# Head rounds of a gated delta net: the convolutions' border terms on GpSimd, one ScalarE operation a panel, and the second transposes in another PSUM bank

## What is computed

```python
def _dn_inputs(p, dn_conv):
    y = jax.nn.silu(_dwconv(p[6], dn_conv)).astype(jnp.float32)      # 3 taps along the tokens, padding 1
    q, k, v = [t.reshape(B, T, DN_HEADS, DN_DIM) for t in jnp.split(y, 3, axis=-1)]
    return (_l2norm(q), _l2norm(k), v) + ...

def _gated_delta_chunked(q, k, v, g, beta, s0):
    ...
    a_mat = jnp.where(strict, jnp.einsum('nbhid,nbhjd->nbhij', kb, kc) * decay_mat, 0.0)
    sol = lax.linalg.triangular_solve(a_mat, rhs, left_side=True, lower=True, unit_diagonal=True)
    ...                      # then a scan over the chunks, for both directions
```

## Time and profile before

| | us |
|---|---|
| time, median of 3 runs (2981.7 to 2985.14) | 2983.79 |
| the profiled execution | 2986.58 |
| its span, first to last instruction | 2984.8 |
| TensorE busy | 2930.5 (98%) |
| VectorE busy | 1928.6 (65%) |
| ScalarE busy | 1460.3 (49%) |
| GpSimd busy | 354.9 (12%) |
| one round, first layer / second layer | 44.85 / 39.2 |

### The profile page before, as it was taken

The page is one execution under the profiler, slowest core; times in us unless marked ns, Lnnn a source line. Parts: engine busy times, 40 slices in busy tenths (PEclk is TensorE's granted clock), DMA queues, the critical chain, the costliest instruction groups (busy, mean ns, idle before and its releaser), DMA issues.

```text
span 2984.8 us, 50450 instructions
## 1 busy us (share of the span) xinstructions
PE 2930.5 (98%) x17768; PEld 2467.4 (83%) x17768; DVE 1928.6 (65%) x3479; ACT 1460.3 (49%) x2497; POOL 354.9 (12%) x272
## 2 busy tenths in 40 slices
PE   7999999999999999999999999999999999999998
PEld 5888888888887788888888888888788889799887
DVE  4777767766535834445665766657777766766777
ACT  5222267777546732224222342223788867644654
POOL 0000024444101000001000000000244421000000
PEclk9999999999999999999999999999999999999999
DMA  7544521111222022233444434444221114155554
GB/s 285 190 168 176 178 93 50 63 63 50 68 95 71 22 99 93 97 106 101 176 151 158 170 123 172 162 141 169 86 71 63 63 63 165 44 176 176 163 183 155
DMA packets 101845, 365.63 MB, mean 122 GB/s; under 512 B 11216, under 2 KB 12880, under 8 KB 101584
## 3 DMA queue, kind: packets, MB, share of 16 engines
q1 hardware_dynamic: 98384, 353.02, 34.6%
q10 hardware_dynamic: 3328, 10.81, 1.0%
HBM read 362.67 MB, written 1.11 MB: 122 GB/s over the span
## 4 chain that ended last, share of the span: by engine, by line
PE 90%; ACT 4%; DVE 3%; issue 2%; DMA 1%; SPq 0%; DVEq 0%; POOL 0%; ACTq 0%; POOLq 0%
PE bank L2123 69%; PE bank L2102 4%; PE bank L2104 2%; PE bank L2681 1%; PE bank L2421 1%; PE bank L2463 1%; PE bank L2396 1%; PE bank L2654 1%; PE bank L2667 1%; PE bank L2393 1%; PE bank L2474 1%; ACT ada_raw L944 1%; PE bank L2453 1%; PE bank L2486 1%; PE bank L2484 1%
## 5 line engine op out<-in xcount | busy, mean ns | idle before, releaser
L584 ACT ACTIVATE whi<-raw 128x1024 fp32r<-128x1024 f32 x518 | 546.7, 1058 | 991.4 <-PE bank L2123 964.1
L2123 PE MATMUL bank<-uh,whi 128*128 128x512 f32 (+1 forms) x2688 | 999.9, 372 | 8.3 <-DVE lmat L1725 2.0
L2123 PE MATMUL bank<-uh,wlo 128*128 128x512 f32 (+1 forms) x2688 | 982.2, 365 | 0.0
L2123 PE MATMUL bank<-ul,whi 128*128 128x512 f32 (+1 forms) x2688 | 972.9, 362 | 0.0
L1310 DVE TENSOR_TENSOR wlo<-raw,whi 128x1024 fp32r<-128x1024 f32 x476 | 583.4, 1226 | 368.6 <-ACT whi L584 353.4
L2123 PEld LDWEIGHTS bank<-uh,whi 128*128 128x128 f32 x2688 | 508.4, 189 | 97.4 <-issue 26.4
L2123 PEld LDWEIGHTS bank<-uh,wlo 128*128 128x128 f32 x2688 | 508.1, 189 | 72.8 <-issue 3.4
L2123 PEld LDWEIGHTS bank<-ul,whi 128*128 128x128 f32 x2688 | 508.4, 189 | 71.6 <-issue 3.8
L2123 PE MATMUL bank<-bh,whi 128*128 128x512 f32 (+1 forms) x930 | 340.1, 366 | 0.8 <-DVE bl L2042 0.8
L2123 PE MATMUL bank<-bl,whi 128*128 128x512 f32 (+1 forms) x930 | 337.6, 363 | 0.0
L2123 PE MATMUL bank<-bh,wlo 128*128 128x512 f32 (+1 forms) x930 | 337.6, 363 | 0.0
(11 more groups left out here) (309 smaller groups left out, 3835.0 us busy)
## 6 DMA issues: line engine op xcount, KB each, us to landing
raw<-stream SPq DMA_DIRECT2D x520, 512.0 KB, 3.3
ada_raw<-stream SPq DMA_DIRECT2D x132, 512.0 KB, 4.3
gc_row<-gc_rows ACTq DMA_DIRECT2D x16, 512.0 KB, 3.7
m<-stream SPq DMA_DIRECT2D x5, 512.0 KB, 13.7
h<-h_in SPq DMA_DIRECT2D x1, 2048.0 KB, 12.2
cst<-consts SPq DMA_DIRECT2D x1, 1104.0 KB, 7.7
lmat<-stream SPq DMA_DIRECT2D x2, 512.0 KB, 11.5
gc_row<-stream SPq DMA_DIRECT2D x2, 512.0 KB, 11.1
```

Source lines behind the costliest of these rows:

```text
L584: act.activation(whi[:, j, :], raw[:, j, :], ACT.Copy).then_inc(hi_ready, 1)
L2123: last = mm(bank[j if to is None else to][:, c0:c1], w(t, a), x[:, t, c0:c1], start=n == 0, stop=n == 3 * kts - 1)
```

## The change

ScalarE scales each whole panel with the inner tokens' bias, in one operation. A new function `edges` of GpSimd then subtracts, at the first and last token of each sequence, the bias times the tap outside (an operation on 128 partitions x 2 sequences x 2 ends), and VectorE's first half waits for it (`edge_ready`) instead of for the tap. The table of bias columns now holds the products themselves, so VectorE's last two operations on it go. GpSimd has the three border operations at three places: between Qt and the tail, between the two IT, and between the two pairs of `low_squares`. Ahead of the rounds the first head's three come first, and in the step of head 0 the next head's come at the same places.

VectorE makes the v convolution's first half after the last mask of level 6 (`at` = 11) instead of between the two, and its second half between the two XT. TensorE's direction-1 transposes of A go to bank 5, whose k transposes ScalarE has copied away; the waits follow: `ktok_ready` before the transposes, `vtok_ready` before the first projection into bank 2, `l_ready` before level 0 of direction 1.

```diff
+                def edges(b, n):
+                    j = (1, 0, 2)[n]
+                    a = c0 // CTX if j == 0 else 0
+                    x = kraw[:, :] if j == 1 else qkv[:, j, :]
+                    ends = x.rearrange("p (s t) -> p s t", s=2)[:, a:2, 0:256:255]
+                    bias = hx[:, j:j + 7:6].rearrange("p (s e) -> p s e", s=1).broadcast_to([128, 2 - a, 2])
+                    pool.wait_ge(E["tap_ready"], 3 * (l * DNH + b) + n + 1)
+                    pool.tensor_tensor(ends, ends, bias, ALU.subtract).then_inc(E["edge_ready"], 1)
@@ GpSimd, step
                         pool.tensor_tensor(Qt[:, d, c0:T], qkv[:, 0, c0:T], eg[:, d, c0:T], ALU.mult).then_inc(E["qt_ready"], 1)
+                    if follow:
+                        edges(b + 1, 0)
                     if after:
                         tail(b - 1)
                     pool.wait_ge(E["kq_ready"], o + 1)
                     for d in range(2):
+                        if follow and d:
+                            edges(b + 1, 1)
                         pool.wait_ge(E["dt_ready"], 2 * o + d + 1)
...
-                        for n in range(2):
-                            low_squares(b + 1, n)
+                        low_squares(b + 1, 0)
+                        edges(b + 1, 2)
+                        low_squares(b + 1, 1)
...
+                for n in range(3):
+                    edges(0, n)
                 masked(l * DNH)
                 step(0, True, False)
@@ ScalarE, prep_tap
-                for lo, hi, e in ((1, CTX - 1, 9), (0, 1, 0), (CTX - 1, CTX, 6)):
-                    last = act.activation(y[:, :, lo:hi], p[:, :, lo:hi], ACT.Identity, scale=hv[:, 5 + 3 * j:6 + 3 * j],
-                                          bias=hx[:, e + j:e + j + 1])
-                last.then_inc(E["tap_ready"], 1)
+                act.activation(y, p, ACT.Identity, scale=hv[:, 5 + 3 * j:6 + 3 * j], bias=hx[:, 9 + j:10 + j]).then_inc(E["tap_ready"], 1)
@@ VectorE, head_vectors
-                dve.tensor_tensor(e[0], e[3], e[0], ALU.subtract)
-                steps.do(dve.tensor_tensor(e[2], e[3], e[2], ALU.subtract))
-                steps.sync()
@@ VectorE, prep_conv, first half
-                    dve.wait_ge(E["tap_ready"], 3 * o + n + 1)
+                    dve.wait_ge(E["edge_ready"], 3 * o + n + 1)
@@ VectorE, first_level
-                    dve.tensor_tensor(c4d(lmat[:, d, :]), c4d(bank[7 if d == 0 else 2][:, :]), bc(ident, TC, 128),
+                    dve.tensor_tensor(c4d(lmat[:, d, :]), c4d(bank[7 if d == 0 else 5][:, :]), bc(ident, TC, 128),
@@ VectorE, head
-                        if follow and at in (3, 7, 10):
+                        if follow and at in (3, 7, 11):
                             prep_conv(l, b, at // 4, second=False)
-                        if follow and at in (5, 9, 11):
-                            prep_conv(l, b, at // 4 - 1 if at < 11 else 2, first=False)
+                        if follow and at in (5, 9):
+                            prep_conv(l, b, at // 4 - 1, first=False)
                 for d in range(2):
                     dve.wait_ge(E["q_sum"], 14 * o + 12 + d + 1)
                     dve.tensor_tensor(c4d(XT[:, d, :]), bc(ident, TC, 128), c4d(bank[4 + d][:, :]), ALU.subtract).then_inc(E["xt_ready"], 1)
+                    if follow and d == 0:
+                        prep_conv(l, b, 2, first=False)
@@ TensorE, output_and_front
-                        pe.wait_ge(E["vtok_ready"], f + 1)
+                        pe.wait_ge(E["ktok_ready"], f + 1)
...
-                        last = pe.transpose(bank[7 if d == 0 else 2][:, sl(c)], AT[:, d, sl(c)], ident)
+                        last = pe.transpose(bank[7 if d == 0 else 5][:, sl(c)], AT[:, d, sl(c)], ident)
@@ TensorE, head
                 level(0, 0)
-                pe.wait_ge(E["l_ready"], 2 * o + 2)
+                pe.wait_ge(E["vtok_ready"], o + 1)
                 pe.wait_ge(E["kq_ready"], o + 1)
                 project(3)
-                pe.wait_ge(E["ktok_ready"], o + 1)
+                pe.wait_ge(E["l_ready"], 2 * o + 2)
                 have(pe, E["eo_ready"], o)
                 level(0, 1)
```

More of the change, by code:

```diff
@@ L284, in build @@
         E = {n: sem(n) for n in (
-            "hv_ready", "hb_ready", "hgc_ready", "tap_ready", "conv_ready", "silu_ready", "hsq_ready", "low_square",
+            "hv_ready", "hb_ready", "hgc_ready", "tap_ready", "edge_ready", "conv_ready", "silu_ready", "hsq_ready", "low_square",
             "l2_sum", "l2_rstd", "kn_ready", "qn_ready", "k_turned", "v_turned", "ktok_ready", "vtok_ready",
```

## The result

The changed kernel takes **2994.93 us**, the median of 8 runs (2993.76 to 2996.76), beside 2984.68 for the kernel before (8 runs, 2981.63 to 2987.42). The ratio is 1.0034, with an interval of 1.0026 to 1.0043: the change costs about 10 us. The prediction was 2993.7. The execution profiled here took 2994.39, its span is 2992.6.

What follows compares the result with a forecast made beforehand. TensorE, busy 98% of the span, bounds the kernel. First layer +8.6, second layer +1.8, ahead of the first round -0.5 sum to +9.9 us, so a median of 2993.7 us; 8-in-10 range 2978 to 3004.

Steps and rivals of the forecast that it cites:

- The mechanism: First-layer rounds: VectorE idles some 2.7 us for GpSimd's third border operation, XT is late, 1.23 us lost a round.
- the 0.41 and 1.0: Level 6 of direction 1 starts sooner: 0.41 us gained a first-layer round, 1.0 a second-layer round.
- the 0.52: Second layer, level 6: 0.52 us gained for the first half by the shorter tap, 0.5 for the second.
- The border operation: GpSimd's 128x2x2 operation: 0.15 us on its queue and 0.20 until done, in no row of the profile.
- Second layer: Its rounds: the 1.0 us gained is spent on the wait for XT; 0.25 lost a round, +1.8 in seven.
- What follows the silu has room: First layer: third silu, table load and logarithms move by the same 1.23 us as XT and have room.
- Bank 5: Direction 1's transposes: the 2.0 us wait for bank 2's read-out moves to L1728's product and ScalarE's copies; counted nothing.
- Ahead of the first round: Second layer, once: GpSimd's products L534 move away from VectorE's L1728, which is freed: -0.5 us.
- I count it like the others: Each layer's first round, where GpSimd starts from another place, counted at the same loss as the other rounds.
- In time: Rival: GpSimd's third border operation is early enough, XT is not late, the gains stand: 2973.4 us, chance 0.10.
- The dear border operation: Rival: four strided elements cost 0.69 us from start to start instead of 0.15: 3016.4 us, chance 0.10.
- The part of the wait: Rival: GpSimd is 0.7 us sooner than counted, so no change: 2983.9 us, chance 0.20.

Runs made afterwards that it cites:

- e3: The changed kernel without any border operation, VectorE waiting for ScalarE's tap as before: 2976.18 us.
- e1: The changed kernel with GpSimd's third border operation between the two operations of the first inner-product pair instead of behind the pair: 2977.14 us.
- e7: The kernel before with only ScalarE's scaling in one operation, the correction of first and last tokens left out: 2978.55 us.
- e6: The kernel before with only the third convolution's halves moved on VectorE, still with ScalarE's three-piece tap: 2977.92 us.
- e2: The changed kernel with both halves of the third convolution behind both XT on VectorE, GpSimd's order unchanged: 2987.35 us.
- e5: The kernel before with only direction 1's transposes in bank 5 and the exchanged waits: 2984.07 us.
- e10: The changed kernel once more, word for word, for a second profile: 2995.20 us.
- e8: The changed kernel with each border operation of a round issued once more, into unused columns ahead of the real one: 3002.94 us.
- e4: The changed kernel with GpSimd's third border operation ahead of the whole first inner-product pair: 2979.38 us.
- e9: The changed kernel with the third border operation between the first pair's operations and both third-convolution halves behind both XT: 2982.40 us.

## Why the prediction was right, step by step

**The mechanism.** VectorE was to idle some 2.7 us, released by GpSimd: 2.82. Counted from the start of Qt, the third border operation was to be done after 14.02 us (588.39 to 602.41) and was after 14.03 (587.71 to 601.74); XT of direction 1 after 16.69, and was after 16.67; the products L2421 after 17.68, and were after 17.64. The loss a first-layer round was to be 1.23 and is 1.21; in the second 0.25, and is 0.24. That the 0.41 and 1.0 are there to be won behind the wait is shown by e3 (44.44 and 38.22, that is 0.42 and 1.00 below before), that the wait takes them by e1. The prediction works out neither the 0.52 nor the 0.5 of the second layer; e7 and e6 measured 0.49 and 0.48. It has GpSimd work "without a gap", but the earlier trace rows show one of 0.16 us ahead of L510: the very place that e1 uses. TensorE was to wait about 1.6 us for XT in the first layer; it waits 0.96 ahead of the products and 0.47 inside them. In the second layer it was to wait about 0.7 and waits 0.48 ahead of them: it came to the products some 0.2 us later than counted, which costs nothing where XT sets the end.

**The border operation** was in no row and was put at 0.15 us on the queue and 0.20 until it is done, from the slope between 256 and 512 columns. The rows say 0.15 to 0.16 and 0.19 to 0.23 (46 of 48). The Trainium skill's Perfetto Trace Analysis (GPSIMD Engine Instruction) warns that spans on that engine don't compose and asks for start-to-start spacing. The trace agrees: the rows overlap by 0.05, and start-to-start spacing gave the end to 0.01 us.

**Second layer.** Of the 0.25 the prediction put 0.09 at the products and the rest at the copies behind the logarithms. The products end 15.62 us after the start of Qt, before 15.51 (2249.94 less 2234.32; 2243.76 less 2228.25): 0.11. The next group, L2449, starts 17.85 after it, before 17.62: 0.23. The copies L991 start 0.23 later as well. Both parts are as forecast.

**What follows the silu has room** was stated for the first layer, and it holds as long as XT is as late as the silu. It isn't a property of the place: e2 took XT out of the wait, and the silu's chain alone makes its first-layer round 0.66 us longer than that of e3 (45.10 against 44.44).

**Bank 5** was counted at nothing and is nothing (e5). The wait for L1728's product came as said. The one for ScalarE's copies behind the output showed once, 0.2 us, in the changed kernel and in e5 (3.0 there, against 2.8 in the kernel before). The 2.8 itself is another wait, at level 6, and went with the shorter tap.

**Ahead of the first round** 0.5 us were to be won. L1739 takes 0.69 at both places, and TensorE doesn't wait for it:

```profile
2150.53 0.69 DVE L1739 TENSOR_TENSOR ada_raw<-lmat,cst 128x512 f16<-128x512 f32 x1
...
2151.86 0.69 DVE L1739 TENSOR_TENSOR ada_raw<-lmat,cst 128x512 f16<-128x512 f32 x1
```

Against the 1.21 of the earlier trace rows, whose neighbour was GpSimd's product; that now stands at 2154.84. The Trainium skill's SBUF — State Buffer (Who interferes with whom) has such a pair block each other. From the last transposes of A to the second level-0 product it is 2.36 us instead of 3.27, so 0.91 won, not 0.5. But the move is not the only way to that: e5 leaves GpSimd's products in their place (2142.53 to 2144.00), they only come sooner against VectorE there, and it has

```profile
2143.90 0.69 DVE L1728 TENSOR_TENSOR ada_raw<-lmat,cst 128x512 f16<-128x512 f32 x1
```

and 2.36 us too. In e6, e7 and e3, which leave them as well, this operation takes 0.69, 0.77 and 0.83. And the stretch from the first layer's last head to the second layer's first is 0.84 us shorter in e5 than in the kernel before, though its rounds are as long. So the 1.21 on which the term rests, and the 0.91, are those of the one profiled execution of the kernel before, and a gain of that size by the change is not shown.

**Where the sum was wrong in its parts.** From the first head's end to the last one's in both layers the profiles are 10.57 us apart:

| stretch | forecast, us | measured, us |
|---|---|---|
| six rounds, first layer | 7.4 | 7.23 |
| first layer's last head to second layer's first | -0.25 | 1.75 |
| six rounds, second layer | 1.5 | 1.59 |

(The -0.25 is 0.25 for a round, less the 0.5 ahead of it.) The middle row is off by 2.0. "I count it like the others" is the step that failed, for the second layer's first round. TensorE there:

```profile
2166.00 0.49 PE L2515 MATMUL bank<-bl,onesr 128*128 128x512 f32 x1 [0.48 <-POOL bl L520]
2167.54 3.33 PE L2434 MATMUL bank<-scr_r,lmat 128*128 128x128 f32 x16 [1.05 <-DVE scr_r L1788]
...
2171.74 1.17 PE L2443 MATMUL bank<-scr_r 128*128 128x128 f32 x8
```

It waits 0.48 us for the low parts and 1.05 for XT, where the other rounds of that layer wait at most 0.48 for XT and not for the low parts: GpSimd begins this chain when a transfer lands, not when VectorE ends a head. And from 2167.54 to L2443 it takes 4.20 us, in the round at 2247.77 only 2.85. Much of that is the granted clock. Stretches of the changed kernel (busy us and count of PE, PEld, DVE, ACT, POOL; then the clock, the DMA share, GB/s):

```profile
2167.50:2169.00 1.50, 1.36 (x9) 1.17 (x10) 1.50 (x3) 0.80 (x2) 0.00 (x0) 0.89 0.00 0
2169.00:2172.00 3.00, 3.00 (x15) 3.00 (x16) 1.12 (x2) 1.82 (x3) 0.00 (x0) 0.50 0.00 0
```

From about 2169 to 2172 TensorE ran at the lower of its two levels, 1.2 GHz, right behind the two waits. e10 shows the same place at 0.50 again, and 1381.29 us for the whole stretch after 1381.24. But e8, the changed kernel with three more small operations a round, has the same two waits there and no fall:

```profile
2170.59 0.50 PE L2517 MATMUL bank<-bl,onesr 128*128 128x512 f32 x1 [0.34 <-POOL bl L522]
2172.29 2.41 PE L2436 MATMUL bank<-scr_r,lmat 128*128 128x128 f32 x16 [1.20 <-DVE scr_r L1790]
...
2175.14 1.07 PE L2445 MATMUL bank<-scr_r 128*128 128x128 f32 x8
```

```profile
2173.70:2176.70 3.00, 3.00 (x25) 2.83 (x25) 1.17 (x2) 2.86 (x5) 0.00 (x0) 1.00 0.00 0
```

From 2172.29 to L2445 it takes 2.85 us, as in the other rounds. So the fall costs 1.35 us of the 2.0 in the two profiles of the changed kernel, but the waits don't bring it by themselves, and what sets it stays open. The longer waits are the rest, less the 0.4 more that was won ahead of them.

In the first layer's first round the loss was 0.49 us, not 1.23: from the masks there (GpSimd, 436.32, before 439.98, both when a transfer landed) to the start of the head's last operation it is 58.32 us, before 57.83. The two errors on first rounds have opposite signs, so that the total of 10.25 lies 0.35 from the forecast is partly luck; the two rows of six rounds are not. The two profiled executions themselves are only 7.8 apart, because the changed kernel ended its first head 3.2 us sooner (495.32, before 498.49). That lies ahead of the heads: TensorE began its first product at 14.22 us instead of 15.34, and of the two only the kernel before fell to the lower clock in this stretch.

```profile
427.00:430.40 3.40, 3.40 (x10) 2.67 (x10) 2.11 (x6) 3.21 (x6) 0.00 (x0) 0.54 0.48 154
```

Neither goes with the change: e1, which has all of it but one place, began at 14.58 and fell there; e5, which has only the bank, began at 14.73 and did not.

**The rivals.** In time (2973.4) is what e3 shows to be there, at 2976.18, and e1 to be reachable, at 2977.14, by a move of two lines. The dear border operation is excluded by its rows. The part of the wait is excluded by the 14.03 us.

## What to carry to other kernels

Before a small operation is handed to an idle engine, place it in that engine's queue and add up what stands ahead of it from the last event that really sets its start: here 0.2 us of work came 14 us after that event, one instruction too late, and turned a gain of some 7 us over 14 rounds (e3) into a loss of 10; one place earlier, in a gap where the engine waits for itself, it cost about 1 (e1). An in-order engine that waits for such an operation holds back everything behind it, so look for all followers (here XT and, through the silu, ScalarE's copies) before moving the wait elsewhere. Parts of a change that free the same wait don't add up, so each has to be priced alone and together.

## What the hardware showed that was not expected

TensorE's clock fell in one profile and not in another after the same work. Two waits of 0.48 and 1.05 us close together were followed by the lower clock in the changed kernel (0.50 from about 2169 to 2172), and so were 0.56 and 1.05 in e10; in e8 waits of 0.34 and 1.20 at the same place were not (1.00). In the kernel before, the clock fell at about 427 us (0.54) with no wait at all, behind 24 products of 8 and 16 columns; the same 24 products stand there in every kernel, and the profiles of e1 to e4, e6 and e9 fall within 1 us of their end too, those of the changed kernel, e5, e7, e8 and e10 don't. What decides it no run here shows. A single profile with such a fall, 1.35 us at the place above, is therefore no evidence for or against a change.

The border operation on four columns took 0.74 us once, ahead of the first layer's first round, beside a VectorE operation with two SBUF inputs (L1324 from 423.00, 1.22 long), where 0.19 to 0.27 is what it takes otherwise:

```profile
423.54 0.74 POOL L510 TENSOR_TENSOR scr<-scr,hv 128x4 f32<-128x4 f32 x1 [2.42 <-ACT scr L828]
```

The second profile of the changed kernel has the same row (423.55, 0.74), and e1, e2, e4 and e9 have it with 0.74 as well. That fits the blocking of the section above, here with GpSimd as the one that waits; no run without the neighbour shows it. The prediction had the new operations only beside VectorE operations with a bank as one input; this one is not. It cost nothing at that place.
